# Square sums of q and k as two fp32r products, the remainder on VectorE, and k's conv taps moved together

## The reference

```python
proj = h @ w_in
qkv = jax.nn.silu(causal_depthwise_conv(qkv, conv_w)).astype(f32)
q, k, v = jnp.split(qkv, [GDN_QK_W, 2 * GDN_QK_W], axis=-1)
# l2norm(x) = x * lax.rsqrt(jnp.sum(x * x, axis=-1, keepdims=True) + EPS)
q = jnp.repeat(l2norm(q.reshape(...)), rep, axis=2) * (dh ** -0.5)
k = jnp.repeat(l2norm(k.reshape(...)), rep, axis=2)
...
t_mat = lax.linalg.triangular_solve(l_mat, eye, lower=True, unit_diagonal=True)
def step(state, inp):
    v_new = uc - wc @ state
    o = qd @ state + qkc @ v_new
    state = state * gl + kd.T @ v_new
```

## Time and profile before

| | us |
|---|---|
| median of 3 runs | 2115.33 (2114.32 to 2115.81) |
| the profiled execution | 2121.64 |
| its span | 2119.8 |
| TensorE busy in the span | 1991.9 (94%) |
| VectorE busy | 1294.2 (61%) |
| ScalarE busy | 864.7 (41%) |
| GpSimd busy | 136.9 (6%) |
| mean granted clock of TensorE | 0.979 of full speed |

### The profile page before, as it was taken

One profiled execution on the slowest core, in us unless ns is written; L12 is line 12 of the kernel. 1 busy time (PEld: TensorE's weight loads), 2 busy tenths in 40 slices (PEclk: granted clock), 3 DMA queues, 4 the chain that ended last, 5 costly groups with the idle time before them and its releaser, 6 DMA issues. The chain is left out here.

```text
span 2119.8 us, 29549 instructions
## 1 busy us (share of the span) xinstructions
PE 1991.9 (94%) x11256; PEld 1635.2 (77%) x11256; DVE 1294.2 (61%) x2447; ACT 864.7 (41%) x1392; POOL 136.9 (6%) x114
## 2 busy tenths in 40 slices
PE   4989999999999999969998999999999899999998
PEld 2667878888887878857776787787787788888877
DVE  6776778796869696659435645454464445733543
ACT  5644353534445353159203244435443337600221
POOL 0020202111120202000000000000000000000000
PEclk8999999999999999989999999999999999999999
DMA  7222323232324233458113220311313116211232
GB/s 280 84 75 69 95 79 105 66 99 74 107 64 112 71 114 96 140 178 282 55 41 127 75 80 27 104 60 50 100 40 100 53 70 225 80 50 50 80 119 80
DMA packets 130251, 204.47 MB, mean 96 GB/s; under 512 B 56852, under 2 KB 88340, under 8 KB 129088
## 3 DMA queue, kind: packets, MB, share of 16 engines
q1 hardware_dynamic: 130112, 202.58, 29.8%
HBM read 156.22 MB, written 42.11 MB: 94 GB/s over the span
## 5 line engine op out<-in xcount | busy, mean ns | idle before, releaser
L795 PE MATMUL p_job<-h_hi,w_hi 128*128 128x512 f32 x768 | 322.3, 420 | 18.5 <-DVE h_lo L185 17.1
L797 PE MATMUL p_job<-h_hi,w_lo 128*128 128x512 f32 x768 | 303.0, 395 | 0.0
L796 PE MATMUL p_job<-h_lo,w_hi 128*128 128x512 f32 x768 | 302.7, 394 | 0.0
L1708 PE MATMUL m_job<-h_hi,m_hi 128*128 128x512 f32 x576 | 247.4, 429 | 5.0 <-issue 4.2
L1710 PE MATMUL m_job<-h_hi,m_lo 128*128 128x512 f32 x576 | 229.6, 399 | 0.0
L1709 PE MATMUL m_job<-h_lo,m_hi 128*128 128x512 f32 x576 | 228.9, 397 | 0.0
L795 PEld LDWEIGHTS p_job<-h_hi,w_hi 128*128 128x128 f32 x768 | 146.3, 190 | 59.3 <-issue 16.2
L796 PEld LDWEIGHTS p_job<-h_lo,w_hi 128*128 128x128 f32 x768 | 146.4, 191 | 35.0 <-issue 7.6
L797 PEld LDWEIGHTS p_job<-h_hi,w_lo 128*128 128x128 f32 x768 | 146.0, 190 | 31.6
L1708 PEld LDWEIGHTS m_job<-h_hi,m_hi 128*128 128x128 f32 x576 | 110.8, 192 | 25.6 <-issue 5.6
L633 ACT ACTIVATE pre<-p_job 128x512 f32<-128x512 f32 x96 | 56.7, 591 | 180.2 <-PE p_job L797 178.5
(11 more groups left out here) (399 smaller groups left out, 4232.9 us busy)
## 6 DMA issues: line engine op xcount, KB each, us to landing
w_raw<-in_w SPq DMA_DIRECT2D x49, 512.0 KB
m_raw<-in_w SPq DMA_DIRECT2D x49, 512.0 KB, 4.2
rows<-grows SPq DMA_DIRECT2D x32, 512.0 KB, 6.5
ada<-in_ada_w SPq DMA_DIRECT2D x8, 1024.0 KB, 5.3
z_scr<-pre SPq DMA_DIRECT2D x16, 512.0 KB, 2.7
o_scr<-oT SPq DMA_DIRECT2D x64, 128.0 KB, 1.8
ob<-o_scr SPq DMA_DIRECT2D x16, 512.0 KB, 5.0
zb<-z_scr SPq DMA_DIRECT2D x16, 512.0 KB, 4.9
```

The source lines that it names most:

```text
L795: nc.tensor.matmul(bank, hi, h_hi[:, k, cut], start=(k == 0), stop=False)
L796: nc.tensor.matmul(bank, hi, h_lo[:, k, cut], start=False, stop=False)
L797: last = nc.tensor.matmul(bank, lo, h_hi[:, k, cut], start=False, stop=(k == KD - 1))
L1708: nc.tensor.matmul(bank, hi, h_hi[:, k, cut], start=(k == 0), stop=False)
```

## The change

It does three things.

1. A square sum is made from two parts. ScalarE squares twice, once into `nsq` in fp32 and once into `sq_r[:, 0]` rounded to fp32r. A new step `nrest` on VectorE subtracts the rounded square from the full one into `sq_r[:, 1]`. TensorE multiplies both parts by a rounded matrix of ones (`ones_r`, copied once at the start) in two fp32r products into the same bank, in the place of one fp32 product.
2. The new step and the others get new counts: for q's first half square 1, remainder 3, sum 5, norm 6; q's second half 6, 8, 11, 14; k's first half 16, 18, 22, 23; its second 23, 25, 28, 30. (Before: 1, 5, 6; 7, 11, 14; 17, 22, 23; 24, 28, 30, without the remainder.)
3. k's four taps all get count 1, so that they stand together after the first slice of the third job, ahead of the split there; before they stood after slices 1, 2, 3 and 4.

`sq_r` shares its place with the third part of `qv`, the second value head. So the first square waits until the value heads of the iteration before are transposed, and the first tap of the third convolution waits until the four sums are done. The room for `ones_r` comes from `cols`, cut from 64 to 48 columns.

The diff, without the declarations of semaphores and buffers:

```diff
             for q in range(TAPS):
-                behind.append((1 + q, ("tap", j, q)))
+                behind.append((1 if j == 1 else 1 + q, ("tap", j, q)))
             behind.append((15, ("silu", j)))
...
-            for m, (square, total, scale) in enumerate(((1, 5, 6), (7, 11, 14), (17, 22, 23), (24, 28, 30))):
+            for m, (square, rest, total, scale) in enumerate(((1, 3, 5, 6), (6, 8, 11, 14), (16, 18, 22, 23), (23, 25, 28, 30))):
                 w = (m // 2, m % 2)
                 behind.append((square, ("nsquare",) + w))
+                behind.append((rest, ("nrest",) + w))
...
+            sq_r = early.enter_context(nc.sbuf_tensor("nsq_r", [P, 2, HALF], F32R))
...
-        cols = sb("cols", [P, NT, 64])
+        cols = sb("cols", [P, NT, 48])
...
                             if i >= 1 and j >= 2:
                                 act.wait_ge(v_ready, 4 * i)
+                            if j == 3 or j < 0:
+                                act.wait_ge(nss_done, 4 * (late(i, j)[0] + 1))
...
+                            if i >= 1:
+                                act.wait_ge(v_ready, 4 * i)
                             nc.scalar.activation(nsq, src, ACT.Square).then_inc(nsq_done, 1)
+                            nc.scalar.activation(sq_r[:, 0, :], src, ACT.Square).then_inc(nhi_done, 1)
...
-                            pe.wait_ge(nsq_done, m + 1)
+                            pe.wait_ge(nlo_done, m + 1)
                             if m >= 1:
                                 pe.wait_ge(nln, m)
+                            else:
+                                pe.wait_ge(ones_set, 1)
                             if i >= 1:
                                 pe.wait_ge(gram_used, 8 * i)
-                            nc.tensor.matmul(p_pre[:], ones[:], nsq, start=True, stop=True).then_inc(nss_done, 1)
+                            nc.tensor.matmul(p_pre[:], ones_r[:], sq_r[:, 0, :], start=True, stop=False)
+                            nc.tensor.matmul(p_pre[:], ones_r[:], sq_r[:, 1, :], start=False, stop=True
+                                             ).then_inc(nss_done, 1)
...
+                        elif s[0] == "nrest":
+                            m = 4 * i + 2 * s[1] + s[2]
+                            dve.wait_ge(nsq_done, m + 1)
+                            dve.wait_ge(nhi_done, m + 1)
+                            nc.vector.tensor_tensor(sq_r[:, 1, :], nsq, sq_r[:, 0, :].bitcast(F32), ALU.subtract
+                                                    ).then_inc(nlo_done, 1)
```

More of the change, by code:

```diff
@@ L372, in stage_deltanet @@
         pre = sb("pre", [P, 2, TAPS - 1 + T])
+        with ExitStack() as early:
+            early.enter_context(nc.sbuf_tensor("qv_first", [P, 2, T], F32))
+            sq_r = early.enter_context(nc.sbuf_tensor("nsq_r", [P, 2, HALF], F32R))
         qv = sb("qv", [P, 3, T])
@@ L400, in stage_deltanet @@
         gbias = sb("gbias", [P, KD])
+        ones_r = sb("b_ones_r", [P, P], F32R)
         cond = kT[:, 0, :]
@@ L424, in stage_deltanet @@
         pad_set = sem("b_pad"); silu_done = sem("b_silu")
-        nsq_done = sem("b_nsq"); nss_done = sem("b_nss"); nln = sem("b_nln"); nexp = sem("b_nexp"); nmul = sem("b_nmul")
+        nsq_done = sem("b_nsq"); nhi_done = sem("b_nhi"); nlo_done = sem("b_nlo"); ones_set = sem("b_ones"); nss_done = sem("b_nss"); nln = sem("b_nln"); nexp = sem("b_nexp"); nmul = sem("b_nmul")
         z_stored = [sem("b_zst0"), sem("b_zst1")]
@@ L682, in _ @@
                             act.wait_ge(g_pe, 1)
-                            nc.scalar.activation(cols[:].rearrange("p a b -> p (a b)"), p_turn[:], ACT.Copy
+                            nc.scalar.activation(cols[:], p_turn[:].rearrange("p (a b) -> p a b", a=NT)[:, :, 0:48], ACT.Copy
                                                  ).then_inc(g_act, 1)
@@ L955, in _ @@
                 nc.vector.memset(adt[32:64, 2:3], 1.0).then_inc(pad_set, 1)
+                dve.wait_ge(keep["const_in"], 32)
+                nc.vector.tensor_copy(ones_r[:], ones[:]).then_inc(ones_set, 1)
                 split(2)
```

## The result

The changed kernel takes 2196.83 us, the median of 4 runs (2196.13 to 2199.99). The kernel before took 2115.57 beside it (4 runs, 2114.32 to 2116.48). The ratio is 1.0388, with a 95% interval of 1.0373 to 1.0404: slower by 81 us. The forecast was 2192, the range 2166 to 2214.

The account below looks back on a forecast made before the run. TensorE, busy 99%, was taken as the bound; stalls for VectorE's remainders add 6 + 7.5 + 3 x 9.4 + 3 x 11.6 = 76.5 us, giving 2198.1 profiled. The median, 6.3 lower, was forecast at 2192, range 2166 to 2214.

Parts of the forecast that it names:

- The queue argument: First sums: VectorE, in order, reaches the remainder only after lanes, taps and split; TensorE waits 10.3 us in iteration 2.
- The wait ahead of iteration 1's merge: Ahead of iteration 1's merge: TensorE's 5.08 us of idle time takes up part of the delay and disappears.
- the clock in odd iterations: Behind each long stall TensorE falls to 1.2 GHz; 1.9 us lost per stall, in odd and even iterations alike.
- its own chain: From one sum through ScalarE's two squares and VectorE's remainder to the next sum: 5.1 us.
- Iteration 0: First iteration: first sum 5.4 us late, 1.9 of clock, about 1.3 given back; +6 us (4 to 8).
- The profiled time: Whole kernel: 2121.64 us plus 76.5 gives 2198.1; the median was taken 6.3 below the profiled execution.
- TensorE sets the time there: work taken from it shortens the stage: Iterations 2 to 7 of the recurrent stage: TensorE, busy 99%, is the bound; cheaper sums save 13.1 us at most.
- Rival (a): Recurrent stage: VectorE keeps pace, all remainders in time, 22 us faster, 2093; chance 4%.
- A square sum hangs on ScalarE alone: Kernel before, square sums: VectorE's being about ten microseconds behind TensorE's place in the plan costs nothing.
- Rival (b): Within each iteration: the stalls come but half of each is taken back elsewhere, +38 us, 2153; chance 6%.
- Rival (c): Fourth sums: short waits also bring the clock down and late splits hold the next job, 2210 and beyond; 12%.
- Rival (d): k's taps: regrouping them does nothing; changes the sum by 4 us at most; no separate chance given.

Follow-up runs that it names:

- the runs with the 42 products: The changed kernel with 42 extra, unused fp32r products on TensorE ahead of the first sums of iterations 1 to 7, run twice: 2194.2 and 2195.65 us.

## Why the prediction was right

Sign, place and size came out as argued; the forecast is 4.8 us below the result, which lies inside the range.

**The queue argument** held to a tenth of a microsecond. Lane group 4 ended at 285.45; taps and split then take 5.69, as counted from the earlier trace rows, and the sum starts 0.74 after the remainder's start, 0.65 in the forecast. The waits of the first sums were forecast at 10.3, 10.75, 10.4 and 5.4 in iterations 2, 3, 1 and 0; they are 10.21, 10.70, 10.30 and 5.29. The wait ahead of iteration 1's merge is gone, as was said. What decided the case was read from the kernel before: the place of VectorE in its list at the moment when TensorE wants the sum.

**Iteration by iteration**:

| | forecast | after | after, second execution |
|---|---|---|---|
| iterations 0 and 1 | 13.5 | 14.0 | 13.1 |
| 2, 4, 6 | 9.4 each | 10.0, 9.6, 9.6 | 9.6, 9.5, 9.5 |
| 3, 5, 7 | 11.6 each | 13.0, 12.3, 12.7 | 12.9, 12.3, 12.7 |
| sum | 76.5 | 81.3 | 79.6 |
| sum, counted from the first sum of iteration 0 | 76.5 | 81.2 | 81.3 |

**The mis-sized term** is the clock in odd iterations. One loss of 1.9 us was taken for every stall. In iteration 2 the slow products end 4.4 us after the sum's start, in iteration 3 they last 5.3 (the third row is its second sum):

```profile
411.83 0.63 PE L805 MATMUL p_job<-h_hi,w_hi 128*128 128x512 f32 x1
412.26 0.51 PE L806 MATMUL p_job<-h_lo,w_hi 128*128 128x512 f32 x1
...
414.23 0.40 PE L839 MATMUL p_pre<-nsq_r,b_ones_r 128*128 128x512 f32 x1
```

The second sum then comes 7.1 to 7.25 after the first there, not 6.44; in even iterations 6.3 to 6.8. Three times 0.7 to 0.8 is 2.1 to 2.4 of the 3.3 us that the odd iterations are over. The term as a whole was about right for another reason than its size: of some 2 us lost behind a stall in an even iteration only about 0.5 reaches the end (up to 1.0 in iteration 2), since the second sum would wait for its own chain anyway. Both the sum with the term (76.5) and without it (67) can be held against the runs with the 42 products, 73.5 and 73.4 counted from the first sum, where the clock doesn't fall behind the stalls of iterations 1 to 7. They lie above 67 for two reasons. The stall of iteration 0 still brings the clock down there (1.9 in the forecast). And three steps of the even iterations take 0.3 to 0.4 longer than was counted: the second sum comes 5.38 after the first and the fourth 5.39 after the third (5.1 counted), the third 8.34 after the second (7.95 counted); in odd ones the same steps take 0.3, 0.2 and 0.1 longer (5.39, 5.29, 8.07). The Trainium skill's rule on the ramp penalty (TensorE: Matmul & The Clock Gate, section "What's actually happening") puts it under 1% of a typical kernel's span. It agrees in size: the 8 us between the two pairs of runs are 0.4% of the span. They are still a tenth of what this change costs.

**Iteration 0** came out right in sum and wrong inside, which is luck. Its fourth sum waits 7.32, which was not forecast, and comes 9.2 us later than before. The run without the remainder has such a wait too (7.53, for ScalarE's second square), so it isn't the remainder's. By the first sum of iteration 1 that is down to 173.96 − 10.30 − 157.37 = 6.3, where 6 was forecast; a wait for the gates, 2.64 before, is 1.31 behind it.

**The profiled time**: 2198.1 was forecast and 2199.99 came, as the rest of the program was 2.9 shorter this time. The median then lay 3.2 below the profiled execution, not 6.3 as before. That gap is chance, and 3 of the 4.8 us are in it. The stage itself came out 4.7 dearer than forecast, and the shorter rest hid 2.9 of that.

**Wrong in the text, though not in the number**: "TensorE sets the time there: work taken from it shortens the stage". The runs without the remainder have every sum 0.35 to 0.41 cheaper and gain nothing (ratios 1.0021 and 1.0002). Rival (a) priced the case with all remainders in time at 22 us faster. There is no such gain with the second square on ScalarE, which rival (a) has too. Its condition was false anyway, so the forecast didn't suffer, but the change without its remainder would have been forecast at least 13 us too fast. A busy share of 99% was read as the bound. It said only that waits were short, not that nothing stood right behind them. The 1.37 us of the earlier trace rows, every second iteration, was the sign: TensorE already touches VectorE's queue there, through k's taps and SiLU. "A square sum hangs on ScalarE alone" holds for q and not for k, as the SiLU of iteration 2 in the kernel before shows:

```profile
280.31 1.06 ACT L703 ACTIVATE kT<-kT 128x1024 f32<-128x1024 f32 x1 [3.96 <-DVE kT L962]
```

The added work was misjudged in the same way: the remainder's 2.6 us per iteration were costed only through the sums that wait for them, but the run with more VectorE work loses 24 to 28 us with nobody waiting for that work.

**Rival (b)** was rightly small: nothing later took the stalls up. **Rival (c)**'s mechanism is partly there: behind a wait of 2.3 us TensorE's products are slow for some time in iterations 2 and 4, and not in iteration 6 (the run without remainder, old taps, and the one with more VectorE work); behind the 2.65 us ahead of iteration 1's fourth sum they are slow in one execution of the changed kernel and not in the other (2.67); behind the waits of 0.52 us in the changed kernel the rows show none. **Rival (d)** was called worth 4 us at most. The regrouped taps do remove the waits of 1.37, but ahead of the remainder they cost 13 to 14, by the forecast's own argument: one more tap stands ahead of the remainder in seven iterations.

**Open**: no run here has the cheaper sums and a VectorE with less to do, or the cheaper sums without the second square, so what fp32r sums could be worth in this stage isn't known. No version run here beats the kernel before.

## What to carry to other kernels

Before a step is put on an engine, read from the trace where that engine stands in its own in-order list at the moment the step's result is wanted; the distance is the wait, and the engine's idle share over a stretch doesn't show it. A bound engine's 99% doesn't mean that cheaper work on it shortens anything: add work to the next engine alone, with nobody waiting, and see whether the time moves. If it does, both have to be reckoned as bounds. That relieving both would gain is to be expected, but no run here shows it.

## What the runs showed of the hardware that was not expected

- After an idle time of 10 us TensorE's products run at the level of 1.2 GHz for 4.4 us in iteration 2 and for 5.3 us in iteration 3 of the same execution, though the idle times differ by only 0.5 us. After 2.29 us of idle time slow products appear too (0.63 instead of 0.39 us), but the same wait doesn't always bring them: behind 2.30 us they came in iterations 2 and 4 and not in iteration 6 of one execution.
- A remainder on GpSimd took 1.42 us in the median and up to 2.75, against 0.69 on VectorE, and VectorE's operations beside it took up to twice their time (826 for 417 ns).
- An fp32 sum of 512 columns costs TensorE 0.86 us and two fp32r products 0.47; the saving came out within 0.02 us of the forecast, and in the two runs without the remainder it was worth nothing (ratios 1.0021 and 1.0002), with a second square on ScalarE beside it.
